# Attention of a hybrid decoder block: the value products of a pair of heads as one run instead of two parts

## The chip, the cores and the metric

The kernel runs on one core of one Trainium2 chip. The metric is the device time of one execution in microseconds (us); the number that counts is the median of several runs. A difference of less than about 0.3% (3.8 us) can't be told from no change for this kernel.

## The reference, cut to what matters

One decoder layer over 1024 tokens and 16 meta tokens, model width 1024. The part that the change touches is the attention over 8 heads of 64, with a forget gate, causal:

```python
u = rms_norm(h, g_mix)
q, k, v, f_logit, b_gate, c_gate, hc = jnp.split(u @ w_in, SPLIT_POINTS, axis=-1)
# q, k: RMS norm per head;  cum: running sum of log sigmoid(f_logit + b_forget)
s = jnp.einsum('bhqd,bkhd->bhqk', qi, k) * Dh ** -0.5 + ci[..., None] - cum_k
p = jax.nn.softmax(jnp.where(allowed, s, MASK_VALUE), axis=-1)
attn = jnp.einsum('bhqk,bkhd->bqhd', p, v)            # the value products
h = h + concat([rms_norm(attn), rms_norm(conv)]) @ w_out
h = h + hierarchical_moe(rms_norm(h, g_ffn), ...)     # top-1 group, top-2 experts of 32
```

## The kernel before

The instruction streams of the five engines are written by hand, with semaphores between them; every engine works in program order. The program has a projection and convolution phase (up to about 378 us of the profiled span), the attention (378 to 629 us), a routing tail, and the experts, whose weights are streamed from memory.

**Units and steps.** The 1024 queries are cut in 8 blocks of 128 (`i`), the 8 heads in 4 pairs (`c`). A unit `u = 4*i + c` is one pair for one block of queries; there are 32 units. The loop over `u` from 0 to 33 is a pipeline of three stages, and I call one pass of it a step. In step `u`, TensorE makes the scores of unit `u` (`scores`, L1120), transposes the probabilities of unit `u-1` (`turn`, L1134) and multiplies those of unit `u-2` with the values (`times_v`, L1152).

**Groups of turns.** A unit of block `i` has `2*(i+2)` blocks of probabilities, transposed in groups of 3 and 4 in turn. Groups 0, 2, 4 go to one PSUM buffer that ScalarE copies out (L1608), groups 1, 3, 5 to another that VectorE copies out (L2106). So group 2 has to wait until ScalarE has copied group 0, and group 4 until it has copied group 2. The number of groups grows from 2 for the early blocks to 6 for the last.

**Value products.** `times_v(u, part, parts)` issues the products of key blocks `n*part//parts` to `n*(part+1)//parts`, for both heads; before, it is called with parts 0 and 1 of 2. Part 0 holds the waits on the copied turns, the last part raises `pv_done`. A product shows in the trace as two matmuls of 64 output rows, so a half of 4 products reads x8. All matmuls of L1152 write PSUM bank `OB`.

**Extras.** What a finished block `r` of queries needs afterwards is spread over the steps that follow, at four places a, b, c, d of a step (tables `PE_EXTRA`, `DVE_EXTRA`, `ACT_EXTRA`; `first_step(r) = 4*r + 6`). On TensorE:

- step 4r+6, d: `M`, the mean square of the attention output (L1165, L1168)
- step 4r+7, c and d: `W0`, `W1`, the two halves of the output projection (L1025 to L1027, 12 products each); VectorE adds them to the residual stream (L1968)
- step 4r+8, c and d: `U0`, `U1`, transposes of the normed stream (L1185), copied out by ScalarE (L1651) and VectorE (L1990)
- step 4r+9, c and d: `L`, the routing logits (L1190), copied out by VectorE into `lgc` (L1997), and `LT`, their transpose (L1193)
- step 4r+11, b: `G`, the rank of each token in its expert (L1207, L1208), read by VectorE (L2037); it falls in the step of `W0` and `W1` of the block after

All extras use one PSUM bank, number 7, so each waits until the one before it was copied out. For block 7, the extras after step 33 are the tail (`PE_TAIL`, `DVE_TAIL`, `ACT_TAIL`). Stretches of useless matmuls (`stream`, L1230) stand where TensorE would have nothing to do.

VectorE and ScalarE go through the same steps. VectorE: place a, `take_scores` of head 0, copy of group 1, place b, `take_scores` of head 1 (both L2094), copy of group 3, place c, copy of group 5, place d. ScalarE: place a, copy of group 0, place b, exponentials of head 0, copy of group 2, place c, exponentials of head 1 (L1615), copy of group 4, place d.

**After the attention.** The queue of SyncE waits for `pv_done` of the last unit and then starts the first expert weights (L725). ScalarE makes their high part (`wg_high`, L1684), VectorE their low part (`wg_low`, L2146); in the order of VectorE the first `wg_low` stands ahead of the addition of `W0` of block 7 (L1968).

Of the kernel before, what the change touches and what calls it, by code (L numbers as in the profile page):

```python
# [101 lines left out]
def first_step(r):  # L102

    return PAIRS * r + PAIRS + 2
# [12 lines left out]
def extras_at(table, step, place):  # L117

    return [(kind, r) for r in reversed(range(NT)) for (rel, at), kind in table.items()
            if at == place and step == first_step(r) + rel and step < UNITS + 2]  # L120
# [82 lines left out]
def turns(u):  # L203


    blocks = [(a, j) for a in range(2) for j in range(u // PAIRS + 2)]
    out = []
    while blocks:
        n = 4 if len(out) % 2 else 3
        out.append(blocks[:n])  # L210
        blocks = blocks[n:]
    return out


def turns_before(u, odd):

    return sum(len(turns(v)[odd::2]) for v in range(u))


def build(nc, x, meta, g_mix, w_in, b_forget, gq, gk, conv_w, g_attn, g_conv, w_out, g_ffn,  # L220
          w_rg, b_rg, w_re, b_re, w_gate, w_up, w_down, out):
    ctx = ExitStack()
    with ctx:
# [776 lines left out]
        def _(pe):  # L1000
# [109 lines left out]
            def scores(u):  # L1110

                i, c = divmod(u, PAIRS)
                if u:
                    pe.wait_ge(scores_taken, 2 * u)
                for b in range(first_key(i), width(i), 512):
                    n = min(width(i) - b, 512)
                    for a in range(2):
                        o = 1024 * a + b - first_key(i)
                        half_rows = slice(HD * a, HD * (a + 1))
                        last = mm(big[:, o:o + n], qT[half_rows, c, P * i:P * (i + 1)],  # L1120
                                  kT[half_rows, c, b:b + n], start=True, stop=True)
                        if b + n == width(i):
                            last.then_inc(scores_made, 1)

            def turn(u, g):

                blocks = turns(u)[g]
                pe.wait_ge(probs_ready, 2 * u + 1 + blocks[-1][0])
                earlier = turns_before(u, g % 2) + g // 2
                if earlier:  # L1130
                    pe.wait_ge(pt_out[g % 2], earlier)
                for m, (a, j) in enumerate(blocks):
                    at = max(0, META + P * (j - 1))
                    last = nc.tensor.transpose(turn_buf(g, len(blocks))[:, P * m:P * (m + 1)],  # L1134
                                               probs[:, u % 2, a, at:at + P], ident[:, :])
                last.then_inc(pt_made, 1)

            def times_v(u, part, parts):

                i, c = divmod(u, PAIRS)  # L1140
                if part == 0:
                    if c == 0 and i:
                        pe.wait_ge(o_taken, i)
                    for odd in range(2):
                        pe.wait_ge(pt_out[odd], turns_before(u + 1, odd))
                n = i + 2
                for j in range(n * part // parts, n * (part + 1) // parts):
                    t = (j - 1) % (NT + 1)
                    for a in range(2):
                        h = 2 * c + a  # L1150
                        m = a * n + j
                        last = mm(ps[HD * a:HD * (a + 1), OB, P * c:P * (c + 1)], v[:, t, HD * h:HD * (h + 1)],  # L1152
                                  pT[u % 2][:, P * m:P * (m + 1)], start=(j == 0), stop=(j == n - 1))
                if part == parts - 1:
                    last.then_inc(pv_done, 1)
# [71 lines left out]
            def stream(bank, n):  # L1227

                for _ in range(n):
                    mm(ps[:, bank, :], ones64[:, :], ones64[:, :].unsqueeze(1).broadcast_to([P, 4, P]),  # L1230
                       start=True, stop=True)
# [63 lines left out]
            for u in range(UNITS + 2):  # L1295
                if u < UNITS:
                    scores(u)
                if u < first_step(0):
                    stream(7, 3)
                for kind, i in extras_at(PE_EXTRA, u, "a"):  # L1300
                    extra(kind, i)
                n = len(turns(u - 1)) if 1 <= u <= UNITS else 0
                for g in range(min(2, n)):
                    turn(u - 1, g)
                if u >= 2:
                    times_v(u - 2, 0, 2)
                for kind, i in extras_at(PE_EXTRA, u, "b"):
                    extra(kind, i)
                if u == META_STEP:
                    extra("MS", NT - 1)  # L1310
                for g in range(2, min(4, n)):
                    turn(u - 1, g)
                for kind, i in extras_at(PE_EXTRA, u, "c"):
                    extra(kind, i)
                if u >= 2:
                    times_v(u - 2, 1, 2)
                for g in range(4, n):
                    turn(u - 1, g)
                for kind, i in extras_at(PE_EXTRA, u, "d"):
                    extra(kind, i)  # L1320
# [1010 lines left out]
```

## Time and profile before

| | us |
|---|---|
| median of 3 runs | 1260.42 (1258.85 to 1263.13) |
| profiled execution, its own time | 1260.95 |
| span of the profiled execution | 1259.2 |
| TensorE busy (matmul) | 1129.4, 90% of the span |
| VectorE busy | 631.9, 50% |
| ScalarE busy | 533.5, 42% |
| time from the start of the attention to the end of its last value product | about 251 |

The span and the run's own time differ by 1.8 us, which lie around the program. In the chain that ended last, TensorE has the largest share; so what counts in the attention is when TensorE's next instruction may start, and who releases it.

### The profile page before, as it was taken

To read this page: it belongs to the slowest core of one execution; us is meant where nothing else is said; L and a number is where in the kernel's file an instruction comes from. 1 tells how busy PE (TensorE), PEld (TensorE's weight loads), DVE (VectorE), ACT (ScalarE), POOL (GpSimd) and SP (SyncE) were. 2 spreads that over 40 slices of the span, in tenths; PEclk is the share of its full clock that TensorE was granted. 3 is DMA by queue.
4 is the path that set the end of the run, shared out by engine and by line. 5 is a ranking of instruction groups with operands and counts; after the bars stand their busy time and mean duration, and the time that the engine had idled before them with its cause. 6 is when DMAs were issued, how large, how long until landed. Compare 5 with 4: busy or idle time off the path is not lost.

```text
span 1259.2 us, 18115 instructions
## 1 busy us (share of the span) xinstructions
PE 1129.4 (90%) x6677; PEld 853.6 (68%) x6677; DVE 631.9 (50%) x909; ACT 533.5 (42%) x804; POOL 216.3 (17%) x256
## 2 busy tenths in 40 slices
PE   6999999999998999998887999999899999989960
PEld 6999988899995666666666886655565555555530
DVE  6422233334335566665577875555545444445526
ACT  7302141143335454454345864554544544444520
POOL 4000001132000111101123112222222212222210
PEclk9999999999999999999998999999999999999985
DMA  9420015333004333222178999999999999999869
GB/s 264 101 68 1 1 48 186 134 108 130 1 1 134 89 97 85 68 80 72 69 302 321 362 370 406 418 424 403 404 391 375 408 389 397 409 389 394 354 245 361
DMA packets 66249, 291.53 MB, mean 232 GB/s; under 512 B 10696, under 2 KB 36328, under 8 KB 53648
## 3 DMA queue, kind: packets, MB, share of 16 engines
q1 hardware_dynamic: 48176, 243.38, 50.8%
q0 software_dynamic: 16720, 42.65, 9.1%
q10 hardware_dynamic: 1296, 4.72, 0.9%
q8 instruction: 38, 0.62, 0.2%
q14 instruction: 19, 0.16, 0.0%
HBM read 270.62 MB, written 37.92 MB: 245 GB/s over the span
## 4 chain that ended last, share of the span: by engine, by line
PE 59%; DMA 21%; DVE 7%; ACT 6%; issue 6%; SPq 1%; DVEq 0%; ACTq 0%; POOLq 0%
DMA wu<-in_w_up 15%; PE ps L1025 9%; PE ps L1027 9%; PE ps L1026 9%; PE ps L1389 4%; DMA wd<-in_w_down 3%; PE ps L1341 3%; PE ps L1343 3%; PE ps L1342 3%; PE ps L1152 3%; PE ps L1120 2%; PE ps L1134 2%; DMA y<-expert_rows 2%; PE ps L1330 2%; DVE probs L2094 1%
## 5 line engine op out<-in xcount | busy, mean ns | idle before, releaser
L2146 DVE TENSOR_TENSOR wu_low<-wu,wu_high 128x2048 fp32r<-128x2048 f32 x36 | 81.1, 2286 | 57.1 <-ACT wu_high L1684 57.1
L1355 PE MATMUL ps<-wg,xa 128*64 128x512 f32 x224 | 102.1, 598 | 0.0
L1355 PE MATMUL ps<-wu,xa 128*64 128x512 f32 x224 | 102.1, 598 | 0.0
L1684 ACT ACTIVATE wd_high<-wd 128x2048 fp32r<-128x2048 f32 x36 | 66.8, 1905 | 81.0 <-DMA wd<-in_w_down 79.2
L2146 DVE TENSOR_TENSOR wd_low<-wd,wd_high 128x2048 fp32r<-128x2048 f32 x36 | 81.2, 2287 | 36.3 <-ACT wd_high L1684 36.0
L1684 ACT ACTIVATE wu_high<-wu 128x2048 fp32r<-128x2048 f32 x36 | 66.9, 1907 | 70.0 <-DMA wu<-in_w_up 70.0
L2146 DVE TENSOR_TENSOR wg_low<-wg,wg_high 128x2048 fp32r<-128x2048 f32 x36 | 81.0, 2288 | 21.0 <-ACT wg_high L1684 21.0
L2249 DVE TENSOR_TENSOR hid<-sil,ps 128x512 f32<-128x512 f32 x18 | 12.3, 685 | 130.3 <-PE ps L1343 130.3
L1684 ACT ACTIVATE wg_high<-wg 128x2048 fp32r<-128x2048 f32 x36 | 66.9, 1908 | 25.3 <-DMA wg<-in_w_gate 24.2
L965 POOL DMA_INDIRECT expert_rows<-yb,idxs x32 | 45.5, 1420 | 164.4 <-ACT yb L1733 126.6
L1025 PE MATMUL ps<-uh,w_high 128*128 128x342 f32 (+1 forms) x208 | 71.4, 343 | 0.0
L1027 PE MATMUL ps<-uh,w_low 128*128 128x342 f32 (+1 forms) x208 | 71.3, 343 | 0.0
L1026 PE MATMUL ps<-ul,w_high 128*128 128x342 f32 (+1 forms) x208 | 71.3, 343 | 0.0
L1389 PE MATMUL ps<-wd,ha 128*64 128x512 f32 x224 | 52.8, 615 | 19.2 <-ACT ha L1727 19.2
L1355 PEld LDWEIGHTS ps<-wg,xa 128*64 128x64 f32 x224 | 28.4, 136 | 54.6 <-issue 52.9
L1377 PE MATMUL ps<-wd_high,hh 128*128 128x512 f32 x144 | 57.8, 401 | 3.5 <-DVE hl L2259 3.2
L1341 PE MATMUL ps<-wg_high,xh_first 128*128 128x512 f32 x128 | 52.8, 413 | 8.4 <-DVE xl_first L2159 8.4
L954 POOL DMA_INDIRECT xg<-u_rows,idxg x32 | 51.8, 1618 | 26.1 <-POOL idxg L951 25.0
L1379 PE MATMUL ps<-wd_high,hl 128*128 128x512 f32 x144 | 56.2, 391 | 0.0
L1378 PE MATMUL ps<-wd_low,hh 128*128 128x512 f32 x144 | 56.1, 390 | 0.0
L1615 ACT ACTIVATE probs<-probs,negmax 128x144 f32<-128x144 f32 (+7 forms) x64 | 50.1, 784 | 12.7 <-DVE negmax L2094 12.5
L1134 PE MATMUL ps<-ident,probs 128*128 128x128 f32 x352 | 52.8, 284 | 1.7 <-ACT pT_odd L1608 1.7
(388 smaller groups left out, 2941.9 us busy)
## 6 DMA issues: line engine op xcount, KB each, us to landing
wg<-in_w_gate SPq DMA_DIRECT2D x32, 2048.0 KB, 17.0
wu<-in_w_up SPq DMA_DIRECT2D x32, 2048.0 KB, 19.1
wd<-in_w_down SPq DMA_DIRECT2D x32, 2048.0 KB, 20.3
u_rows<-u POOLq DMA_DIRECT2D x16, 512.0 KB, 6.3
y<-expert_rows SPq DMA_DIRECT2D x16, 512.0 KB, 12.1
raw_c<-in_w_in SPq DMA_DIRECT2D x5, 1024.0 KB, 5.3
xin<-in_x SPq DMA_DIRECT2D x8, 512.0 KB, 10.0
zx<-in_x POOLq DMA_DIRECT2D x4, 1024.0 KB, 7.1
```

Source lines behind the costliest of these rows:

```text
L1025: mm(o, a_high, b_high, start=(k == 0), stop=False)
L1026: mm(o, a_high, b_low, start=False, stop=False)
L1027: return mm(o, a_low, b_high, start=False, stop=(k == last))
L1134: last = nc.tensor.transpose(turn_buf(g, len(blocks))[:, P * m:P * (m + 1)], probs[:, u % 2, a, at:at + P], ident[:, :])
L1341: mm(o, xh[s][:, k, :], wh[m][:, k, :], start=(k == 0), stop=False)
L1355: last = mm(ps[HALF * n:HALF * (n + 1), 7, :], xa[:, k, :], raw[m][:, 1, k, :], start=(k == 0), stop=(k == KT - 1))
L1377: mm(o, hh[:, k, :], wh["d"][:, r, :], start=(k == 0), stop=False)
L1378: mm(o, hh[:, k, :], wl["d"][:, s, r, :], start=False, stop=False)
L1379: last = mm(o, hl[:, k, :], wh["d"][:, r, :], start=False, stop=(k == FT - 1))
L1389: last = mm(ps[HALF * j:HALF * (j + 1), 5 + j, :], ha[:, k, :], wd[:, 1, k, 512 * j:512 * (j + 1)], start=(k == 0), stop=(k == FT - 1))
L1684: A(flat_half(wh[m][:, :, :], n), flat_half(raw_kf(m, s), n), ACT.Copy).then_inc(w_high[m], 1)
L2146: return V.tensor_tensor(flat_half(wl[m][:, s, :, :], n), flat_half(raw_kf(m, s), n), flat_half(wh[m][:, :, :], n).bitcast(F32), ALU.subtr ...
```

## The change

The two calls of `times_v` in the loop over steps become one call behind the first two groups of turns. The second half of the value products thus moves ahead of place b, of groups 2 and 3 and of place c. No instruction is added or removed, and the orders of VectorE, ScalarE, GpSimd and SyncE stay as they are (their lines behind L1315 move up by 2).

```diff
                 for g in range(min(2, n)):
                     turn(u - 1, g)
                 if u >= 2:
-                    times_v(u - 2, 0, 2)
+                    times_v(u - 2, 0, 1)
                 for kind, i in extras_at(PE_EXTRA, u, "b"):
                     extra(kind, i)
...
                 for kind, i in extras_at(PE_EXTRA, u, "c"):
                     extra(kind, i)
-                if u >= 2:
-                    times_v(u - 2, 1, 2)
                 for g in range(4, n):
                     turn(u - 1, g)
```

TensorE in step 17 (block 2's routing logits). The names: `probs` the probabilities to be turned, `pT_odd` the turned ones, `u2T` and `wr` the operands of `L`, `lgc` that of `LT`:

```order
-L1152 MATMUL ps<-pT_odd,v 64x128 x4
+L1152 MATMUL ps<-pT_odd,v 64x128 x10
 L1134 MATMUL ps<-ident,probs 128x128 x5
 L1190 MATMUL ps<-u2T,wr 40x128 x8
-L1152 MATMUL ps<-pT_odd,v 64x128 x6
 L1193 MATMUL ps<-ident,lgc 128x40
```

The six products that stood between `L` and `LT` stand ahead of the turns now. The other steps with `L` and `LT` read the same way, and those with `W0` and `W1` or `U0` and `U1` lose the products between these two extras.

TensorE in steps 32 and 33, the end of the attention (`u_156` is the normed stream of block 6, the operand of `U0` and `U1`):

```order
 L1134 MATMUL ps<-ident,probs 128x128 x7
-L1152 MATMUL ps<-pT_even,v 64x128 x8
+L1152 MATMUL ps<-pT_even,v 64x128 x18
 L1134 MATMUL ps<-ident,probs 128x128 x7
 L1185 MATMUL ps<-ident,u_156 128x128 x4
-L1152 MATMUL ps<-pT_even,v 64x128 x10
 L1134 MATMUL ps<-ident,probs 128x128 x4
 L1185 MATMUL ps<-ident,u_156 128x128 x4
-L1152 MATMUL ps<-pT_odd,v 64x128 x8
+L1152 MATMUL ps<-pT_odd,v 64x128 x18
 L1190 MATMUL ps<-u2T,wr 40x128 x8
-L1152 MATMUL ps<-pT_odd,v 64x128 x10
```

In step 32 the ten products move from behind `U0` to ahead of groups 2 and 3; in step 33 the last products of the attention stand ahead of `L` instead of around it.

## Rows read from the trace of the kernel before

**Rows 1.** The page, part 4: shares of the chain that ended last.

```profile
PE 59%; DMA 21%; DVE 7%; ACT 6%; issue 6%; SPq 1%; DVEq 0%; ACTq 0%; POOLq 0%
```

**Rows 2.** Timeline of PE, step 14: start, duration, what [idle before it <- releaser].

```profile
452.61 0.66 PE L1152 MATMUL ps<-pT_even,v 128*64 128x128 f32 x8
453.20 0.55 PE L1134 MATMUL ps<-ident,probs 128*128 128x128 f32 x3
453.68 0.88 PE L1152 MATMUL ps<-pT_even,v 128*64 128x128 f32 x12
454.48 1.16 PE L1165 MATMUL ps<-ident,l 128*128 128x128 f32 x8
```

**Rows 3.** Timelines of PE and DVE, step 17 and the end of step 29.

```profile
478.58 1.83 PE L1190 MATMUL ps<-u2T,wr 128*40 128x128 f32 x15
...
481.11 0.25 PE L1193 MATMUL ps<-ident,lgc 40*128 40x40 f32 x1
...
480.56 0.28 DVE L1997 COPY lgc<-ps 40x128 f32<-40x128 f32 x1 [0.77 <-PE ps L1190]
...
592.51 0.28 DVE L1997 COPY lgc<-ps 40x128 f32<-40x128 f32 x1
...
592.93 0.23 PE L1193 MATMUL ps<-ident,lgc 40*128 40x40 f32 x1 [1.27 <-DVE lgc L1997]
```

**Rows 4.** Timelines of PE and DVE, step 31, and W1 of step 11.

```profile
605.64 0.96 PE L1134 MATMUL ps<-ident,probs 128*128 128x128 f32 x7
607.97 0.50 PE L1025 MATMUL ps<-woh,aTh 128*128 128x512 f32 x1 [1.37 <-DVE rk L2037]
...
610.92 1.31 PE L1152 MATMUL ps<-pT_odd,v 128*64 128x128 f32 x20
612.16 0.66 PE L1134 MATMUL ps<-ident,probs 128*128 128x128 f32 x4
613.80 0.50 PE L1025 MATMUL ps<-woh,aTh 128*128 128x512 f32 x1 [0.98 <-DVE h1b L1968]
...
607.11 0.69 DVE L2106 COPY pT_even<-ps 128x512 f32<-128x512 f32 x1
...
435.18 0.50 PE L1025 MATMUL ps<-woh,aTh 128*128 128x512 f32 x1 [0.20 <-DVE h1b L1968]
```

**Rows 5.** Timelines of PE and ACT, step 20: U1, and the exponentials of head 1.

```profile
506.75 0.66 PE L1185 MATMUL ps<-ident,u 128*128 128x128 f32 x4 [0.98 <-DVEq L1984]
...
505.11 0.95 ACT L1615 ACTIVATE probs<-probs,negmax 128x784 f32<-128x784 f32 x1 [1.04 <-DVE negmax L2094]
```

**Rows 6.** Timeline of PE, step 32.

```profile
617.56 1.09 PE L1152 MATMUL ps<-pT_even,v 128*64 128x128 f32 x16
619.86 0.95 PE L1134 MATMUL ps<-ident,probs 128*128 128x128 f32 x7 [1.21 <-ACT pT_odd L1608]
...
621.36 1.31 PE L1152 MATMUL ps<-pT_even,v 128*64 128x128 f32 x20
622.60 0.66 PE L1134 MATMUL ps<-ident,probs 128*128 128x128 f32 x4
```

**Rows 7.** Timelines of PE, DVE, the SP queue and ACT, step 33 and the tail.

```profile
625.80 1.80 PE L1190 MATMUL ps<-u2T,wr 128*40 128x128 f32 x15
...
628.86 0.69 DVE L1952 COPY ot<-ps 128x512 f32<-128x512 f32 x1 [0.82 <-PE ps L1152]
...
641.88 0.69 DVE L1968 TENSOR_TENSOR h1b<-ps,h1b 128x512 f32<-128x512 f32 x1
...
640.75 0.40 PE L1027 MATMUL ps<-woh,aTl 128*128 128x512 f32 x1
...
628.86 0.33 SPq L725 DMA_DIRECT2D wg<-in_w_gate  x1
...
636.62 3.72 ACT L1684 ACTIVATE wg_high<-wg 128x2048 fp32r<-128x2048 f32 x2 [2.54 <-DMA wg<-in_w_gate]
```

**Rows 8.** Window of 5 us: length, PE, PEld, DVE, ACT, POOL busy, granted clock, DMA share, GB/s.

```profile
555.00:560.00 5.00, 5.00 (x38) 4.31 (x38) 2.75 (x13) 1.91 (x4) 0.00 (x0) 0.66 0.14 26
```

## The prediction, written before the changed kernel was run

> **What bounds the kernel now.** I read the chain that ended last first: TensorE has 59% of it [rows 1], and VectorE, the next in busy time, works for half of the span. So the change can act only by moving the moment at which TensorE gets on. It neither adds nor removes an instruction. The second question is therefore, for each step, what a half of the value products (here: Vb) now stands beside, and what it stood beside before: where Vb filled a wait, the wait opens; where a wait stood ahead of Vb's old place, Vb now fills it. I read this from the timelines of TensorE, VectorE and ScalarE, with the wait in brackets.
>
> **What a run of products costs.** From the start of a run to the start of the next there are 0.59 us for x8 (452.61 to 453.20), 0.80 for x12 (453.68 to 454.48) [rows 2] and 1.24 for x20 (610.92 to 612.16) [rows 4]. That is 0.055 per matmul and about 0.15 once per run, whatever stands behind it. Joining two halves should save the 0.15 of one run in every step where TensorE itself is what the next work waits for. In numbers below, Vb moved ahead delays what follows by 0.055 a matmul: 0.44, 0.66, 0.88, 1.10 us for x8, x12, x16, x20; taken away from its old place it frees 0.59, 0.80, 1.03, 1.24.
>
> **Steps with L and LT (9, 13, 17, 21, 25, 29): a loss.** In step 17, L is copied by VectorE at 480.56, and LT starts at 481.11, after Vb [rows 3]. The bound behind Vb is read at step 29, where LT waits in the open: copy at 592.51, LT at 592.93, so 0.42 from the start of the copy [rows 3]. In step 17 this bound stood at 480.98, hidden by Vb. Now L and its copy come 0.66 later, and LT at 480.56 + 0.66 + 0.42 = 481.64, 0.53 later than before; the scores of the next step are queued behind LT and go with it, and VectorE and ScalarE wait for those. Read the same way: steps 9 and 13 lose 0.44 each, step 21 0.54. In step 25 group 4 of the turns still stands between L and LT and leaves 0.17; in step 29 LT hangs on VectorE's copy of group 5, and TensorE reaches that group 0.15 earlier: -0.15. Sum +2.0 us.
>
> **Steps with W0 and W1 (7, 11, 15, 19, 23, 27, 31).** W0 waits for VectorE (1.37 us in step 31, for `rk`, the copy of G) [rows 4]. One would think that Vb, now ahead of it, fills this wait for nothing. But VectorE copies group 3 of the turns before `rk`, and group 3 now comes later. In step 31 the turns start 1.10 later, so group 3 ends at 605.64 + 0.96 + 1.10 = 607.70 in place of 606.60; VectorE, which took it at 607.11 [rows 4], takes it at 607.75, 0.64 later, and W0 starts 0.64 later, at 608.61. From W0 to the turns behind it there were 2.95 to Vb and 1.24 of Vb; without Vb group 4 starts at 611.56 in place of 612.16: -0.60, and W1's wait of 0.98 on the sum of W0 stays as it is. In the other steps nothing or only a short group stands between W0 and W1, and W1 has the same sum as a floor: in step 11 it waits 0.20 for it behind Vb already [rows 4], so that Vb's going opens the wait and W1 starts no earlier. Steps 7, 11 and 15 have no group 3: W0 and W1 start when they did, 0. Step 19 loses 0.21, step 23 0.45 (0.60 at W0, 0.15 back at W1), step 27 0.42 (0.77 and 0.35). Sum +1.1 - 0.6 = +0.5 us.
>
> **Steps with U0 and U1 (8, 12, 16, 20, 24, 28).** U1 waits until ScalarE has copied U0, and ScalarE does that only behind the exponentials of head 1, which start at 505.11 in step 20 after a wait of 1.04 for VectorE [rows 5]; U1 follows at 506.75. VectorE's way there doesn't pass the moved products (group 3 comes behind the scores that it takes). U0 itself waited about 0.5 for the normed stream and now has Vb in that wait. So the half moves from one wait into the other and U1 stays: 0, and +0.1 in step 8, where ScalarE has almost no slack. Sum +0.1 us.
>
> **Steps with M (10, 14, ... 30).** Nothing stands between groups 2, 3 and Vb, so only a run is saved, 0.15 in each of four steps: -0.6. In steps 26 and 30 group 4 now follows group 3 at once and has to wait for ScalarE's copy of group 2, which eats the saving. VectorE's routing work there starts up to 0.9 later, behind group 3, but it has 0.7 to 0.8 us of idle time before it is asked for.
>
> **The end of the attention: a gain.** Step 32 has no scores and no exponentials. Its groups 2 and 3 wait 1.21 us for ScalarE behind the first half [rows 6]; whole, the products take 0.15 + 36 x 0.055 = 2.13 and end at 617.56 + 2.13 = 619.69, inside this wait, so the turns start at 619.86 still. Behind U0 the x20 are gone: group 4 starts at 621.36 in place of 622.60 [rows 6], and its copy, U0's copy and U1 come with it: -1.24. In step 33 all products now precede L. The last product ends at about 625.9 in place of 628.8; L, which started at 625.80, starts at 625.76, and VectorE, which takes L before the attention output `ot`, takes `ot` at about 627.9 in place of 628.86 [rows 7]: in all -1.0.
> The queue of SyncE starts the first weights at the last product, 628.86, and ScalarE waits for them until 636.62, 7.76 later [rows 7]; behind that hang `wg_low` and the sums of W0 and W1 on VectorE, the latter at 641.88 [rows 7], though TensorE's last matmul of W1 began at 640.75 and took 0.40 [rows 7], so that its result was ready about 0.7 earlier. The weights now start 2.9 us earlier and the chain of them is off the path; the sum of W1 then follows TensorE's W1, 1.7 earlier than before. Everything behind (routing, gather, experts, whose weight loads wait for the routing) follows this sum: -1.7 for steps 32, 33 and the tail together.
>
> **The sum.** +2.0 + 0.5 + 0.1 - 0.6 - 1.7 = +0.3 us, against the profiled execution's own 1260.95 us: 1261.2. The profiled one lies 0.5 above the median of the runs shown, 1260.42; on that footing 1260.7 us. Bounds: if the opened waits in the steps with L are paid in full and nothing is saved by joining runs, the attention costs 4.2 instead of 2.0; if none of the delays before step 32 passes on, it costs 0 and the end brings -1.7. The median itself is uncertain by about 1.5 us either way, as the three runs spread from 1258.85 to 1263.13.
>
> **Rivals.**
> (1) Joining two runs saves nothing: the 0.15 is not per run but is paid for other reasons, and goes along with the moved half. Then Vb delays by 0.59 to 1.24 and not by 0.44 to 1.10: the L steps lose 2.8, the W steps 1.0, U 0.3, M +0.1, end -1.5: +2.7, 1263.1 us. For it: I know the 0.15 only from runs that have another kind of work on each side. Against: it is the same behind first and second halves, of which only first ones hold waits.
> The Trainium skill, TensorE: Matmul & The Clock Gate, "Step-by-step: what each phase is for", says that the emptying of the array of one matmul overlaps the filling by the next, and that 128 columns follow each other at 55.6 ns; the per-matmul figure agrees with the trace's 0.055, but by the overlap alone a run would have no fixed cost and joining would bring nothing, which is this rival.
> (2) The fall of the clock goes. Once in the attention TensorE's granted clock drops from full speed (2.4 GHz) to half: the window from 555 to 560 has a mean grant of 0.66 [rows 8], right behind the 8 narrow products of 16 columns of step 26, and it costs 5 x 0.34 = 1.7 us of work. Now the whole run of products stands ahead of the narrow ones, and the light stretch is preceded by twice as much dense work. If the clock then stays, 1259.0 us. Whether it does can't be read here.
> (3) Slower: the clock falls more often. The waits of a step are now less broken up: between L and LT and between W0 and W1 TensorE stands still where it had products. Each further fall costs like the one seen, 1.7 us. It decides, that is makes the kernel slower by more than 3.8 us, from the first one on in company of (1) (+4.4, 1264.8 us), or from three on alone (0.3 + 5.1, 1265.8 us). Against it: the opened waits are below 1 us each, and before, waits of 1.3 us (W0) passed without a fall.
> (4) The end gives more, or the attention's losses are taken up by waits further on (VectorE or ScalarE late anyway), so that together with (2) more than 3.8 us are gained: below 1256.6.
>
> **How the numbers follow.** Forecast 0.55, (1) 0.17, (2) 0.15, (3) 0.08, (4) 0.05. Likeliest 1260.7. The range runs from (2) with the spread of a median, 1256.8, to (1) with it and a little more, 1265.0; it leaves out (4) and most of (3). About 0.3%, 3.8 us, is what a measurement can tell from no change; faster by more than that 0.05, within it 0.85, slower 0.10.
>
> **What would show it.** In the profile after: LT with a wait of about 0.3 to 0.5 on `lgc` in steps 9 to 25; W1 waiting 0.8 on `h1b` in steps 7 to 27, W0 less than before; in step 32 no wait of group 2 on ScalarE; the first weights issued 2.9 us nearer to the start of step 32; the sum of W1 right behind TensorE. The step from the start of the attention to step 32 should be 1.9 us longer, and from there to the routing 1.7 shorter. The prediction is wrong if the runs of x16 to x36 don't follow 0.15 + 0.055 a matmul, if the clock has more or fewer falls in the attention, or if the experts' part changes its length.

## The result and the profile after

| | kernel before | changed kernel |
|---|---|---|
| median | 1261.45 us (1258.38 to 1265.58, 20 runs) | 1264.14 us (1261.46 to 1268.25, 20 runs) |
| ratio | | 1.0029, 95% interval 1.0019 to 1.0038 |

So the changed kernel is slower by 3.7 us of 1261 (2.4 to 4.8), going by the ratio; the two medians differ by 2.7 us and the two means by 3.5. The forecast was 0.3 us slower. The time lies inside the range given, but the loss is clear of noise and some ten times the one forecast. The profiled execution of the changed kernel took 1267.91 us (span 1266.2), near the upper end of its 20 runs, so its trace shows more than the usual loss; two more traces of it are used below.

TensorE's share and its clock on the page of the changed kernel (part 1, and the clock row of part 2, tenths of full speed in 40 slices of 32 us):

```profile
PE 1131.1 (89%) x6677; PEld 856.9 (68%) x6677; DVE 632.4 (50%) x909; ACT 534.1 (42%) x804; POOL 214.1 (17%) x256
...
PEclk8999999999999999989997999999999999999995
```

The 8 in the middle is in the attention (538 to 570 us), the 7 (665 to 696) behind it. In the kernel before no slice of the attention is under 9, and the slice in the place of the 7 is an 8. (The 8 at the very start is a fall from 16.9 to 24.0, at a time when the attention starts no later for it: 379.22 against 379.13.)

**The steps one by one.** The start of the first scores of each step, taken from TensorE's timeline, gives the length of each step. Against the kernel before (us; clock falls are dealt with below, and steps in which one trace has a fall were read from a trace that has none there):

```
step with  L, LT    9 +0.44   13 +0.43   17 +0.54   21 +0.54   25 +0.17   29  0.00
forecast              +0.44      +0.44      +0.53      +0.54      +0.17      -0.15
step with  W0, W1  11 -0.04   15 -0.02   19 +0.17   23 +0.48   27 +0.45
forecast               0          0         +0.21      +0.45      +0.42
step with  U0, U1   8 +0.07   12 +0.01   16  0.00   20  0.00   24  0.00   28  0.00
forecast              +0.1        0          0          0          0          0
step with  M       10 -0.35   14 -0.34   18 -0.37   22 -0.38   26 +0.87   30 +0.50
forecast              -0.15      -0.15      -0.15      -0.15       0          0
```

Here are rows of the changed kernel to set beside those of before. Step 17 (timeline of PE), answering to [rows 3]:

```profile
477.74 1.15 PE L1152 MATMUL ps<-pT_odd,v 128*64 128x128 f32 x18
478.82 0.76 PE L1134 MATMUL ps<-ident,probs 128*128 128x128 f32 x5
479.52 1.94 PE L1190 MATMUL ps<-u2T,wr 128*40 128x128 f32 x16
481.93 0.23 PE L1193 MATMUL ps<-ident,lgc 40*128 40x40 f32 x1 [0.47 <-DVE lgc L1995]
```

LT now waits in the open, 0.47 us for VectorE's copy of the logits. Step 31 (timelines of PE and DVE), answering to [rows 4]:

```profile
614.91 0.96 PE L1134 MATMUL ps<-ident,probs 128*128 128x128 f32 x7
616.78 0.50 PE L1025 MATMUL ps<-woh,aTh 128*128 128x512 f32 x1 [0.91 <-DVE rk L2035]
...
619.66 0.60 PE L1134 MATMUL ps<-ident,probs 128*128 128x128 f32 x4
621.23 0.50 PE L1025 MATMUL ps<-woh,aTh 128*128 128x512 f32 x1 [0.98 <-DVE h1b L1966]
...
615.91 0.69 DVE L2104 COPY pT_even<-ps 128x512 f32<-128x512 f32 x1 [0.55 <-PE ps L1134]
```

VectorE, which came to group 3 late before, now stands idle 0.55 us for it: W0 hangs on the moved turns. Its wait shrank from 1.37 to 0.91 only, but the products behind it are gone. Step 32 and the tail (PE, DVE, ACT), answering to [rows 6, 7]:

```profile
627.25 0.95 PE L1134 MATMUL ps<-ident,probs 128*128 128x128 f32 x7
628.19 0.63 PE L1185 MATMUL ps<-ident,u 128*128 128x128 f32 x4
628.65 0.72 PE L1134 MATMUL ps<-ident,probs 128*128 128x128 f32 x4
...
635.03 0.67 DVE L1950 COPY ot<-ps 128x512 f32<-128x512 f32 x1
...
647.48 0.69 DVE L1966 TENSOR_TENSOR h1b<-ps,h1b 128x512 f32<-128x512 f32 x1
...
642.23 3.71 ACT L1682 ACTIVATE wg_high<-wg 128x2048 fp32r<-128x2048 f32 x2 [1.99 <-DMA wg<-in_w_gate]
```

Groups 2 and 3 no longer wait (1.21 us before), and from the start of step 31 (601.32 before, 609.50 after) to the last sum of W1 (641.88, 647.48) there are 37.98 us in place of 40.56: 2.6 less. Two more traces of the changed kernel have 38.33 and 38.04, a second one of the kernel before 40.75.

So without the clock the attention is 3.2 us longer and the end 2.5 shorter: +0.7 us. The greater part of the 3.7 is what the next rows show, windows of 1 us of the changed kernel (PE, PEld, DVE, ACT, POOL busy, granted clock, DMA share, GB/s), and the timeline of PE over them:

```profile
504.00:505.00 1.00, 1.00 (x14) 0.71 (x9) 1.00 (x2) 0.37 (x3) 0.00 (x0) 1.00 0.00 0
505.00:506.00 1.00, 0.58 (x5) 0.34 (x4) 1.00 (x4) 0.62 (x2) 0.90 (x2) 1.00 0.31 37
506.00:507.00 1.00, 0.00 (x0) 0.00 (x0) 0.42 (x4) 1.00 (x3) 0.19 (x1) 1.00 0.84 205
507.00:508.00 1.00, 0.63 (x6) 0.47 (x6) 0.00 (x0) 0.26 (x1) 0.00 (x0) 1.00 0.94 262
508.00:509.00 1.00, 1.00 (x5) 0.60 (x6) 0.69 (x1) 0.00 (x0) 0.00 (x0) 0.72 1.02 418
509.00:510.00 1.00, 1.00 (x6) 0.35 (x2) 0.00 (x0) 0.00 (x0) 0.00 (x0) 0.50 0.92 347
```

```profile
504.95 0.63 PE L1185 MATMUL ps<-ident,u 128*128 128x128 f32 x4
507.37 0.66 PE L1185 MATMUL ps<-ident,u 128*128 128x128 f32 x4 [1.79 <-DVEq L1982]
507.95 2.55 PE L1120 MATMUL ps<-kT,qT 64*128 64x512 f32 x8
510.44 1.65 PE L1134 MATMUL ps<-ident,probs 128*128 128x128 f32 x7
```

In step 20 TensorE stands still for 1.79 us between U0 and U1, and then its granted clock falls from full (2.4 GHz) to half (1.2): the scores take 2.55 us instead of 1.59, the turns 1.65 instead of 0.98. I call such a stretch at half clock a fall. Summed over windows of half a microsecond, each fall costs 1.71 us of full-speed work. This execution has four in the attention, from 508.4, 546.0, 563.0 and 590.4; three of them begin behind U1 of steps 20, 24 and 28. The profile of the kernel before has one.

The stretch from the first scores of the attention to the last sum of W1 gives the whole of it: 262.75 and 262.97 us in the two traces of the kernel before, with one fall each, and 268.26, 265.35 and 265.14 in the three of the changed kernel, with four, two and two. The means differ by 3.4 us: 0.7 without the clock, and 1.7 falls more at 1.71. What follows this stretch takes 614.9 to 619.0 us in these five traces, whichever the kernel.

### The profile page after: what moved, and what is told of

The parts are those of the page before. It is cut to its first block, busy times and chain, and to the rows that moved or that the text cites. A ratio compares the mean times of both kernels' runs of the same rounds, so it can differ in the third digit from the quotient of the medians.

```text
span 1266.2 us, 18115 instructions
## 1 busy us (share of the span) xinstructions
PE 1131.1 (89%) x6677; PEld 856.9 (68%) x6677; DVE 632.4 (50%) x909; ACT 534.1 (42%) x804; POOL 214.1 (17%) x256
## 4 chain that ended last, share of the span: by engine, by line
PE 61%; DMA 20%; DVE 7%; issue 6%; ACT 5%; SPq 1%; DVEq 0%; ACTq 0%; POOLq 0%
DMA wu<-in_w_up 15%; PE ps L1025 9%; PE ps L1027 9%; PE ps L1026 9%; PE ps L1387 4%; PE ps L1339 4%; PE ps L1341 3%; PE ps L1340 3%; PE ps L1120 3%; PE ps L1134 3%; PE ps L1152 2%; PE ps L1353 2%; DMA y<-expert_rows 2%; DMA wd<-in_w_down 2%; PE ps L1328 2%
## 5 line engine op out<-in xcount | busy, mean ns | idle before, releaser
L951 POOL COPY idxg<-tab 128x1 int32 x32 | 19.3, 602 | 228.3 <-PE ps L1328 219.2
L954 POOL DMA_INDIRECT xg<-u_rows,idxg x32 | 48.8, 1524 | 26.1 <-POOL idxg L951 25.0
```

## Experiments

All ratios are against the kernel before, run between the variants on the same chip; in us they are of 1261. A ratio need not be the quotient of the two medians beside it; where the two differ much it is said.

**split_u: the changed kernel without its edit in the steps with U0 and U1.**

```diff
+                whole = u >= 31 or u % 4 != 0
                 if u >= 2:
-                    times_v(u - 2, 0, 1)
+                    times_v(u - 2, 0, 1 if whole else 2)
...
+                if u >= 2 and not whole:
+                    times_v(u - 2, 1, 2)
```

> As the changed kernel, but the products are cut in two again in the six steps with U0 and U1 that have scores (8, 12, ... 28), so that their second half stands between U0 and U1 as before. Theory A: the extra falls of TensorE's clock come from the wait in front of U1, 1.8 us long since nothing stands in it, with the narrow scores behind it. Then the attention shows one fall as before and the time is the kernel before +0.3 us (the sum of the prediction without clock), between -1 and +1.5. Theory B: the falls come from the opened waits in general (LT, W1). Then this kernel still has 3 to 4 falls in the attention and is 2.5 to 3.5 us above the kernel before, as the changed one is. Theory C: the extra time isn't the clock but runs that don't join: +2.7 us with one fall.

Measured: 1263.15 us against 1261.06, ratio 1.0016 (1.0007 to 1.0025), +2.0 us (0.9 to 3.2). In its trace the falls behind U1 are gone, as A says, but the time is still above A's range. The trace has one fall, in steps 26 and 27, of double length (3.42 us lost, from 557.6 to 564.5). That led to theory D.

**only_u: the kernel before with one run in the steps with U0 and U1 alone.** The same edit with `whole = u < 31 and u % 4 == 0`.

> The kernel before with the products in one run in the six steps with U0 and U1 alone (8, 12, ... 28). By the steps of the prediction these are worth +0.1 us. Theory A: the falls of the clock in the steps right behind (21, 25, 29) are all there, 2 to 3 more than before at 1.7 us each, and the time is +2.5 to +4 us. Theory B or C: +0.1 us, clock as before.

Measured: 1264.65 us, ratio 1.0039 (1.0026 to 1.0052), +4.9 us (3.3 to 6.6; +3.6 by the medians), for steps whose lengths changed by nothing in the trace where the clock stayed (steps 8, 12, 16, 20 and 24: +0.07, 0, 0, 0, 0). B and C, which gave +0.1, fall. But its size isn't explained: its traced execution was the fastest of the six and has two falls in the attention where the kernel before has one, which makes the stretch to step 31 1.65 us longer. The timeline of PE in its step 20:

```profile
504.40 0.63 PE L1185 MATMUL ps<-ident,u 128*128 128x128 f32 x4
506.81 0.66 PE L1185 MATMUL ps<-ident,u 128*128 128x128 f32 x4 [1.78 <-DVEq L1985]
507.39 2.29 PE L1120 MATMUL ps<-kT,qT 64*128 64x512 f32 x8
```

**filler_u: the changed kernel with useless work in that wait.**

```diff
                 for kind, i in extras_at(PE_EXTRA, u, "c"):
                     extra(kind, i)
+                if 12 < u < 32 and u % 4 == 0:
+                    pe.wait_ge(scores_taken, 2 * u + 1)
+                    stream(0, 5)
```

> The changed kernel with five useless matmuls of 512 columns (about 1.3 us) between U0 and U1 in steps 16, 20, 24 and 28, on PSUM bank 0, whose scores VectorE has taken by then. They lie inside the wait of 1.8 us, so they delay nothing by themselves. Theory A: TensorE is busy again in front of U1 and the falls of steps 21, 25, 29 go: +0.3 us against the kernel before (-1 to +1.5). Theory B: 3 to 4 falls as in the changed kernel, +2.5 to +3.5.

Measured: 1262.24 us, ratio 1.0010 (0.9998 to 1.0022), +1.3 us (-0.3 to 2.8). With twenty added matmuls the kernel loses about 2.4 us less than the changed one, though the two intervals overlap a little. Its step 20:

```profile
504.66 0.63 PE L1185 MATMUL ps<-ident,u 128*128 128x128 f32 x4
505.04 1.39 PE L1230 MATMUL ps<-ones 128*128 128x512 f32 x5
507.08 0.66 PE L1185 MATMUL ps<-ident,u 128*128 128x128 f32 x4 [0.64 <-DVEq L1988]
507.66 1.59 PE L1120 MATMUL ps<-kT,qT 64*128 64x512 f32 x8
```

U1 starts 2.42 us after U0, as without the filler (2.42 in the changed kernel, 504.95 to 507.37), and the scores run at full speed (1.59). No fall lies behind U1 in its trace; like split_u it has a double one in steps 26 and 27.

**m_end: one run only where it gains.** `whole = u >= 31 or (u % 4 == 2 and u < 26)`.

> One run only where the trace of the changed kernel shows a gain: the steps with M without group 4 (10, 14, 18, 22: 0.35 us shorter each there) and the end (steps 31 to 33 and the tail: 2.6 us shorter there). All other steps as before. Theory A and C: -1.4 - 2.6 = -4.0 us, clock as before. If the gain at the end only showed against a start that was late (weights and routing meet other limits), -1.4 us.

Measured: 1258.27 us against 1261.06, ratio 0.9980 (0.9968 to 0.9992), -2.5 us (-4.0 to -1.0): faster than both kernels, though short of the 4.0 expected. Its trace shows where the rest is: steps 10, 14, 18 and 22 are 0.34 shorter each, but step 19 is 0.11 and step 23 0.44 longer, for VectorE's routing work starts later behind group 3 in step 22, so that VectorE comes 0.40 later to the scores of step 23 and to `rk`, for which W0 waits (W0 starts 6.26 us after the scores, 5.86 before); and the end gives 2.2 (38.35 against 40.56).

**split_u26: split_u with step 26 cut in two as well.** `whole = u >= 31 or (u % 4 != 0 and u != 26)`.

> As split_u, and step 26 (the one with the narrow products of 16 columns, L1200) is cut in two again as well. In the trace of split_u step 26 was 1.2 us longer than before and step 27 1.1, with a fall of the clock of twice the length (3.4 us of work lost against 1.7). Theory D: a second source of the extra time is step 26, where M now waits for VectorE's `metas` and no products stand behind the narrow ones. Then this kernel is +0.2 us against the kernel before (-1 to +1), with one fall of 1.7 in the attention. Rival: the double fall of split_u and filler_u is chance, and this kernel stays at +2.0.

Measured: 1261.50 us against 1261.53, ratio 0.9996 (0.9985 to 1.0007), -0.5 us (-1.9 to 0.9). With the edit undone in six steps with U0 and U1 and in step 26, and kept everywhere else, the kernel can't be told from the kernel before. Its trace has no fall in the attention.

**only_26: the kernel before with one run in step 26 alone.** `whole = u == 26`.

> The kernel before with the products of step 26 alone in one run. The steps of the prediction gave 0 for it. Theory D: +0.6 us for the waits of group 4 and of M, and 1.7 for the longer fall: +1.5 to +2.5. Rival (chance): 0 to +0.6.

Measured: 1262.74 us, ratio 1.0017 (1.0003 to 1.0030), +2.1 us (0.4 to 3.8). The interval holds D's value and the rival's upper end. The waits that D names are there (timeline of PE, step 26):

```profile
553.89 2.18 PE L1200 MATMUL ps<-kT,qT 64*128 64x16 f32 x16
556.00 0.98 PE L1134 MATMUL ps<-ident,probs 128*128 128x128 f32 x7
557.22 0.41 PE L1134 MATMUL ps<-ident,probs 128*128 128x128 f32 x2 [0.23 <-ACT pT_odd L1609]
558.15 1.16 PE L1165 MATMUL ps<-ident,l 128*128 128x128 f32 x8 [0.53 <-DVE metas L2025]
```

They make the step 0.87 us longer than without them (compared with only_u, neither with a fall there). This execution had no fall in step 26, so the longer fall is seen in the traces of split_u and filler_u (3.4 us lost in each) but not in this one. That the undivided products of step 26 bring the longer fall isn't shown.

**only_l: one run in the steps with L and LT alone.** `whole = u < 31 and u % 4 == 1`.

> The kernel before with one run of products only in the steps with L and LT that have scores (9, 13, ... 29). The prediction gave these six steps +2.0 us (0.44, 0.44, 0.53, 0.54, 0.17, -0.15); the changed kernel's trace, with its falls of the clock taken off, has 0.44, 0.43, 0.54, 0.54, 0.17, 0. So +2.1 us, clock as before. If the opened waits in front of LT bring falls of the clock too (theory B), +4 or more.

Measured: 1262.45 us, ratio 1.0013 (0.9998 to 1.0028), +1.6 us (-0.3 to 3.5), with 2.1 expected. The interval leaves out the +4 of theory B: the opened waits of 0.5 us in front of LT cost about what they measure.

**m_end_ms: m_end, with the narrow products of step 26 on either side of groups 2 and 3.**

```diff
                         if a:
+                            for g in (2, 3):
+                                turn(META_STEP - 1, g)
                             pe.wait_ge(first_meta, 1)
...
-                for g in range(2, min(4, n)):
+                for g in range(2, min(4, n) if u != META_STEP else 2):
```

> m_end, and in step 26 the narrow products are cut in two, the halves on either side of groups 2 and 3 of the turns. If a light stretch is what drops the clock, the fall that the kernel before has in step 26 goes in most executions: -1.5 us more than m_end's -2.5, so about -4 us. If not, -2.5.

Measured: 1257.81 us against 1261.53, ratio 0.9977 (0.9966 to 0.9987), -2.9 us (-4.3 to -1.6). It can't be told from m_end, and its trace has a fall from 557.9 in step 26 still. That the narrow products are what drops the clock there isn't shown.

**Four more traces.**

> The changed kernel once more, for its trace. Theory A: of its falls of the clock in the attention, at least one again begins behind the wait in front of U1 of steps 16 to 28, none of the kernel before does. Chance alone: the falls lie anywhere.

> As after_b: a third trace of the changed kernel, same expectation.

> The kernel before once more, for its trace: one or two falls in the attention, in step 26 or at the wait in front of W0, none behind the wait in front of U1.

> only_u once more, for its trace. Its first one was the fastest of six executions and had two falls behind the wait in front of U1. Theory A: two or three again, of steps 16, 20, 24 and 28.

These single executions took 1260.59 us (after_b), 1262.72 (after_c), 1262.41 (before_b) and 1263.52 (only_u_b). With two falls in the attention, after_b is faster than the median of the kernel before: the rest of the program varies by more than a fall from one execution to the next.

The window from 500 to 512, which holds the end of step 20 and the start of step 21, of the kernel before, before_b, only_u, only_u_b, the changed kernel, after_b and after_c, in this order (columns as above, the granted clock is the third from the right):

```profile
500.00:512.00 12.00, 10.45 (x91) 7.17 (x90) 8.58 (x18) 7.32 (x16) 1.68 (x3) 1.00 0.54 186
500.00:512.00 12.00, 10.46 (x86) 6.90 (x86) 7.78 (x16) 6.39 (x14) 1.68 (x3) 1.00 0.51 187
500.00:512.00 12.00, 10.21 (x77) 6.82 (x79) 7.32 (x15) 6.39 (x14) 1.67 (x3) 0.86 0.59 187
500.00:512.00 12.00, 10.22 (x76) 7.02 (x77) 7.42 (x16) 6.38 (x14) 1.68 (x3) 0.86 0.52 186
500.00:512.00 12.00, 10.21 (x70) 6.47 (x68) 6.79 (x14) 5.60 (x13) 1.68 (x3) 0.86 0.54 184
500.00:512.00 12.00, 10.22 (x77) 6.71 (x77) 7.11 (x15) 5.83 (x13) 1.68 (x3) 0.86 0.55 186
500.00:512.00 12.00, 10.22 (x75) 6.72 (x77) 7.10 (x15) 5.74 (x13) 1.68 (x3) 0.86 0.55 187
```

12 x 0.14 is 1.7 us, one fall. In after_b and after_c it begins with U1 itself, whose four transposes then take 1.12 us in place of 0.66 (timeline of PE of after_b):

```profile
506.79 1.12 PE L1185 MATMUL ps<-ident,u 128*128 128x128 f32 x4 [1.78 <-DVEq L1982]
```

So the scores behind U1 aren't needed for a fall to begin. Over all traces, falls in the attention by place:

```
                               behind U1 of step   in step 26   at W0 (step 11, 23)
                                20   24   28
products whole between U0, U1
  changed kernel                 x    x    x          x
  after_b, after_c               x         x
  only_u, only_u_b               x         x
products or filler between them
  before, m_end                                       x
  split_u, filler_u                                   x (double)
  only_l                                              x          x
  m_end_ms                                            x          x, x
  before_b                                                       x
  split_u26, only_26
```

Five of five executions with the bare wait fall at U1 of steps 20 and 28; none of nine with something in it does. In steps 12 and 16, whose waits in front of U1 are 1.35 and 1.54 us in the changed kernel, none of the five falls. The other places come and go from one execution to the next with the same code.

The whole executions point the same way: the part of the span that the granted clock leaves out (one minus its mean, times the span) is 32.0 us in the mean of 64 executions of the kernel before, 34.7 in 20 of the changed one, 37.7 in 6 of only_u, 34.1 in 11 of split_u, and 31.9 in 12 of filler_u, each but the first uncertain by about 1. (m_end has 33.3, m_end_ms 33.0, split_u26 32.0, only_26 33.8, only_l 30.8.) But this sum doesn't say where, and not all of it costs time: over the 64 executions of the kernel before, an execution with 1 us more left out is only 0.4 us slower. Two places lie outside the attention. The first trace of the changed kernel and both of only_u have the fall at the start (3.42 us left out), the other eleven don't, and it delays nothing. And between the last sum of W1 and 701 us these three have five falls each, the others three or four. From that sum to the first expert product with `wg` it takes 115.8 to 116.9 us with three falls, and 116.8 to 118.1 with four or five. So part of what only_u loses, and perhaps of what the changed kernel loses, lies behind the attention, in code that the edit doesn't touch; why isn't shown.

## Why the prediction was wrong

**The sum without the clock was nearly right.** It had +0.3 us, and the traces have +0.7.
- L and LT: +2.0 forecast, +2.1 measured, step by step the same to 0.01 but for step 29, where the saved run doesn't reach LT. only_l confirms it as a whole.
- W0 and W1: that Vb in front of W0 fills no wait, because VectorE copies group 3 ahead of `rk`, came out in every step (+1.0 against +1.1), and step 31 is shorter as told (group 4 starts 10.16 after the scores, 10.84 before). In step 23 a second cause lies hidden beneath it: m_end, with step 23 as before, pays 0.44 there for the edit of step 22. The prediction took this delay of VectorE's routing work for nothing, as 0.7 to 0.8 us of idle time would take it up; they don't (0.40 is left over). In the changed kernel group 3 is later still (W0 6.45 after the scores), so that the number came out all the same.
- M: -0.6 forecast, -0.1 measured, from two errors against each other. In steps 10 to 22 the gain is 0.35 and not 0.15: the turns of group 2 now stand next to M's transposes, which are the same kind of work, so that two runs are saved. In steps 26 and 30 I let the waits of group 4 eat the saving, and they cost more: in step 30 group 5 waits for VectorE's copy of group 3 as well, and in step 26 M waits 0.53 us for `metas`, a copy that stands behind group 3 on VectorE and that I had not followed. These two steps are +0.9 and +0.5.
- The end: -2.3 forecast (step 31 with it), -2.2 to -2.8 measured. The number fits, the path in part. In the first trace, counted from the start of step 31, the first weights are started 4.0 us earlier (23.58 after, 27.54 before), but ScalarE has them 9.15 us later and not 7.76, so only 2.6 of it arrives; in all three traces of the changed kernel the sum of W0 still stands right behind `wg_low` on VectorE, and that of W1 1.10 behind it, as before. The chain of the weights isn't off the path, as the prediction has it; it moved along with TensorE, whose W1 ends 2.0 earlier.
- A run of x36 takes 2.11 us (603.48 to 605.59 in step 30), with 2.13 forecast, so that joining does save the 0.15: rival (1) is out. By the overlap that the Trainium skill describes (TensorE: Matmul & The Clock Gate, "Step-by-step: what each phase is for") joining would save nothing; the trace differs, and the measurement decides.

**The step that failed** is "So the half moves from one wait into the other and U1 stays: 0". It is right for the time of U1 (0.00 in steps 12 to 28) and wrong as a price. Before, the half stood inside the stretch of about 2.4 us from the start of U0 to that of U1 and left a wait of 0.98; taken out, TensorE stands still for 1.8 us in step 20 (2.25 in step 28), and the clock falls. Two such falls in every execution seen, 1.7 us each, are +3.4; against them the fall in step 26 is missing in four of these five. 0.7 + 3.4 is 4.1, and the fall that is mostly gone in exchange brings it down toward the 3.7 measured: over the stretch up to the last sum of W1, three traces of the changed kernel and two of the kernel before differ by 3.4 in the mean.

That 1264.14 lies inside the range all the same is luck: the upper bound, 1265.0, was set for rival (1), which didn't happen.

**Rival (3) was the right one and was underrated**, at 0.08. It named the mechanism and the price of a fall, 1.7, which is what was measured. But it looked for the falls between L and LT and between W0 and W1, whose waits are 0.5 and 1.0 us, and left out the longest wait that the change opens, the one in front of U1. Its argument against, that waits of 1.3 us in front of W0 pass without a fall, was read from one execution: before_b, only_l and m_end_ms have a fall at W0 of step 11, behind the same wait of 1.31 or 1.32 us, with that step's code unchanged. And the point from which it decides was put too high: fewer than two falls more, with the rest of the sum, make a difference that 20 runs of each can tell. The Trainium skill has a like pattern (TensorE: Matmul & The Clock Gate, "A second HAM failure mode: psum-queue depth-cycling"): where the engine idles briefly and often between groups of matmuls, the clock goes back and forth between its two levels. The traces here agree that short waits can do it (1.8 us in step 20, 1.71 us lost); how often they must come isn't shown here. The prediction should have compared, for each step, the longest stretch in which TensorE would stand still before and after, and not only the end of the step.

**Rival (2)** happened in part: in four of five traces with whole products between U0 and U1 the fall of step 26 is gone. But split_u and filler_u have it at double length with the same order in step 26, so the order of dense and narrow work doesn't decide alone.

## What to carry over

When work is moved out of a wait on TensorE, two prices are due: what becomes late, and how long the engine now stands still. The first can be zero and the second not: five useless matmuls in the bare wait of four steps took some 2.4 of the 3.7 us back. Look for the longest stretch without work that a change creates, and compare it with the longest that the trace already survives, in more than one execution. And an edit that is applied in every step of a pipeline need not be worth the same in each; here it pays in steps 10, 14, 18 and 22 and at the end and costs elsewhere, and the version that keeps only these (m_end, 0.9980) beats both kernels.

## What the runs showed of the hardware

- A fall of the granted clock, from 2.4 to 1.2 GHz, costs 1.71 us of full-speed work in the attention of all traces, and where two join they cost 3.42. A bare wait of 1.8 us (step 20) or one of 2.25 us behind two turns (step 28) had a fall at its end or just behind it in 10 of 10 cases, one of 1.80 in step 24 in 1 of 5, and those of 1.35 and 1.54 in steps 12 and 16 in 0 of 10. What makes the difference between steps 20 and 24 stays open.
- The same code at the same place falls in one execution and not in another (before in step 26, before_b in step 11), so one profile can't settle the clock's share. The mean of the granted clock over many executions tells how much was left out, to about 1 us, but not where: it counts falls that delay nothing, such as the 3.42 us at the start of three traces.
- Joining neighbouring runs of like matmuls saves 0.15 us a run, and it does so for different lines too (turns next to M's transposes).
